# Two gate projections of a mixer: their high and low weight parts ordered pairwise

## The chip, the cores and the metric

The kernel runs on one core of one Trainium2 chip. The metric is the time of one execution on the device in microseconds. Three runs of the kernel before gave 1438.70, 1439.01 and 1439.03, a median of 1439.01.

## The reference

The input x has 256 tokens of 1024 features, all in float32. Two layers of a first kind and one of a second kind follow each other. A layer of the first kind is: a feed-forward block (SwiGLU, inner width 2816), a mixer, and a second feed-forward block. The mixer is what the change touches:

```
h = rms_norm(x, mix_norm)
z = h @ w_in                      # u, q, k, v of 512 columns each, and gl of 2 x 1024
y_pool = multiscale_pool(u, pool_w, pool_scale)
q, k = rope(rms_norm(q)), rope(rms_norm(k))
y_attn = moba_attention(q, k, v)  # 8 heads of 64, causal
gates = sigmoid(gl + b_gate).reshape(B, S, 2, D)
merged = gates[:, :, 0] * (y_pool @ w_branch_pool) + gates[:, :, 1] * (y_attn @ w_branch_attn)
x = x + merged @ w_out
```

With 256 tokens and attention blocks of 256, the attention is plain causal attention over the 256 tokens.

## The kernel before

**Precision.** Every weight tile (128 x 1024 elements) and every activation is split in a high part (float32r) and a low part (what the high part leaves). A product is high x high + high x low + low x high. ScalarE makes the high part of a tile (`whi`, line 1092), VectorE the low one (`wlo`, line 1625). There are 8 raw buffers and 6 of each part. The order of the tiles is a list, and all engines follow it. A semaphore `tile` counts the tiles that TensorE has done with. ScalarE waits for it before it overwrites a buffer, and tables (`HI_LEAD`, `LO_LEAD`) say how many tiles ahead the splits run: for the gate tiles four (ScalarE) and three (VectorE).

**Stages.** Eight stages: `L0f1`, `L0`, `L0f2`, `L1f1`, `L1`, `L1f2`, `M`, `Mf`. `L0` and `L1` are mixers one and two, `M` is a mixer of the second kind, the others are feed-forward blocks.

**A gate.** The gate projections give 2 x 1024 features, for 256 tokens. They are computed by eight feature blocks of 128 (f), each with two gates (j = 0 and 1; called A and B here). `wide_block` of one gate is `high_part` and then `low_part` (lines 556 to 574):

- `high_part` waits for the tile's high weights and issues eight matmuls of 128 x 512 (line 559): the moving operand holds the high and the low activations side by side, so columns 0 to 255 of the bank get high x high and columns 256 to 511 high weights x low activations.
- `low_part` waits for the low weights and issues eight matmuls of 128 x 256 (line 566) into columns 0 to 255, and the last one raises `tile`.

Each gate has a PSUM bank of its own, taken in turn from four (`claim`, banks 0 to 3). A claim waits until VectorE has added up the gate that had the bank before. When a gate is done, ScalarE copies its columns 256 to 511 to `gates` (line 1282, `gate_low`), VectorE adds columns 0 to 255 (line 1921), and ScalarE applies a tanh (line 1288).

**Attention beside it.** The attention of the mixer is spread over the gate blocks by `tick()`. TensorE's `high_part` calls it after its sixth matmul and `low_part` after its last, so a feature block has four ticks. At each call `attention` looks up what falls due (`attention_beat`): the heads come as four pairs. For a pair whose scores are at tick n:

- n: `scores` on TensorE (line 743); VectorE's maxima (lines 1772, 1773); ScalarE's four exponentials (lines 1241, 1242)
- n+2, n+3: `sums` of the first and the second head on VectorE (reciprocal, line 1785; scaling, lines 1791 and 1792)
- n+4, n+5: `turn_p` on TensorE, three transposes of the first and of the second head (line 754). They wait for the scaling of their head, and those of the second head also for ScalarE's eviction of the first (line 1249)
- the product with v (line 769) for two pairs at once, 12 ticks after the scores of the first of them

Counted from the first tick of the first feature block, the scores of the four pairs are at ticks 0, 6, 12 and 18.

ScalarE and VectorE have a fixed program of their own in the same beats. For each gate in turn VectorE does: split of the weight tile three ahead, two ticks, wait for ScalarE's copy, add. ScalarE does: split of the tile four ahead, two ticks, copy of the gate, tanh of the gate before. These two programs are written gate by gate:

```
for f in range(KD):
    for j in range(2):
        ahead(T[f"{tag}g{j}{f}"])
        tick()
        tick()
        g = gates[:, (2 * f + j) * S:(2 * f + j + 1) * S]
        E.wait_ge("g_low", 16 * l + 2 * f + j + 1)
        e.tensor_tensor(g, g, bank[...][:, 0:S], ALU.add).then_inc(sem["g_sum"], 1)
```

The feed-forward stages use the same two functions for their blocks. There most blocks have the parts in the order high, high, low, low (line 711), and the last block of a stage has two `wide_block`s (lines 717, 726).

Of the kernel before, what the change touches and what calls it, by code (L numbers as in the profile page):

```python
# [302 lines left out]
def build_program(nc, x_in, wstream, gains, const_in, par_in, out, cat, pat, plan):  # L303
    K = Counts(plan)
    T, DONE, SI = K.T, K.DONE, K.SI

    with ExitStack() as ctx:
# [98 lines left out]
        def jobs1(l):  # L406

            out_ = []
            for h in range(8):
                c = h // 2  # L410
                out_.append(dict(
                    q=lambda a, b_, c=c, r=64 * (h % 2): qT1[r:r + 64, c * S + a:c * S + b_],
                    k=lambda a, b_, c=c, r=64 * (h % 2): kT1[r:r + 64, c * S + a:c * S + b_],
                    sc=scq.rearrange("p (a h) -> p h a", a=2)[:, h, :], nsc=nscq.rearrange("p (a h) -> p h a", a=2)[:, h, :],
                    v=lambda s, h=h: v1[:, s * 512 + h * 64:s * 512 + h * 64 + 64],
                    gate=None, pair=c, first=True, last=True))
            return out_
# [91 lines left out]
        def pe_program(E):  # L509
# [11 lines left out]
            def claim(name):  # L521
                b, s, v = K.BANK[name]
                E.wait_ge(s, v)
                return bank[b]
# [31 lines left out]
            def high_part(j, b, tick=None):  # L556
                E.wait_ge("w_hi", SI[j] + 1)
                for k in range(KD):
                    e.matmul(b[:, :], hi_of(j)[:, k * P:k * P + P], hx[:, k * 2 * S:k * 2 * S + 2 * S], start=k == 0, stop=False, skip_group_check=True)  # L559
                    if tick and k == 5:  # L560
                        tick()

            def low_part(j, b, tick=None):
                E.wait_ge("w_lo", SI[j] + 1)
                for k in range(KD):
                    ins = e.matmul(b[:, 0:S], lo_of(j)[:, k * P:k * P + P], hiT(k), start=False, stop=k == KD - 1, skip_group_check=True)  # L566
                ins.then_inc(sem["tile"], 1)
                if tick:
                    tick()

            def wide_block(j, b, tick=None):

                high_part(j, b, tick)
                low_part(j, b, tick)
# [31 lines left out]
            def first_group(n, g):  # L606

                groups = a_group(512)
                for i, (k0, m) in enumerate(groups):
                    E.wait_ge("xlo", 4 * n + (1 if k0 < 4 else 2))  # L610
                    last = i == len(groups) - 1
                    group_part(g, 512, T[f"{g}{k0}"], k0, m, 0, claim((g, 0)), (lambda: norm_transposes(n, 1, (0,))) if last else None)
                norm_transposes(n, 1, (1,))
                for i, (k0, m) in enumerate(groups):
                    done = 4 * n + (3 if k0 < 4 else 4)
                    if i:
                        E.wait_ge("xlo", done)
                        group_part(g, 512, T[f"{g}{k0}"], k0, m, 1, claim((g, 1)))
                    else:
                        E.wait_ge("xhi", 4 * n + 3)  # L620
                        group_part_low_last(g, 512, T[f"{g}{k0}"], k0, m, 1, claim((g, 1)), done)

            def group(g, n, tick):
                for k0, m in a_group(n):
                    for a in range(2):
                        group_part(g, n, T[f"{g}{k0}"], k0, m, a, claim((g, a)))
                        tick()
# [155 lines left out]
            def attention(m, b, first, js, before):  # L783
                for what, i in attention_beat(m, b, first, len(js)):
                    if what == "scores":
                        if i == 0:
                            before(0)
                            before(1)
                        scores(m, i, js)
                    elif what == "turn":  # L790
                        turn_p(m, i)
                    elif what == "out":
                        if i == 0:
                            before(2)
                        attend(m, i, js)
                    elif what == "post":
                        attend_compressed(i)

            def turn4(srcs, b):
                for k, s in enumerate(srcs):  # L800
                    ins = e.transpose(b[:, k * P:k * P + P], s, ident)  # L801
                return ins
# [19 lines left out]
            def mixer1(s, l):  # L822
                tag = STAGES[s]
                js = jobs1(l)
                beat = 0

                def turn_qk(a, isq):
                    if isq:
                        E.wait_ge("rp_add", 4 * l + 2 + a + 1)
                        E.wait_ge("kt_ev", 2 * l + a + 1)  # L830
                    else:
                        E.wait_ge("x", 4 * (s - 1) + a + 1)
                        E.wait_ge("rp_add", 4 * l + a + 1)
                        E.wait_ge("ld_c", 16)
                    turn4([ro[:, a * 512 + c * P:a * 512 + c * P + P] for c in range(4)], side[a]).then_inc(sem["qkt_t"], 1)

                def pool_diff(g):
                    E.wait_ge("u_ev", 2 * l + 2)
                    E.wait_ge("ld_pm", 16 * l + 16)
                    E.wait_ge("ld_pw", 16 * l + 16)  # L840
                    if g < 2:
                        E.wait_ge("kt_ev", 2 * l + g + 1)
                    else:
                        E.wait_ge("qt_ev", 2 * l + g - 1)
                        E.wait_ge("dT", 4 * l + g - 1)
                    b, pm = side[g % 2], poolm[:, g * 384:g * 384 + 384]
                    reach = P + 2 ** (g + 1)
                    e.matmul(b[:, 0:reach], us[:, g * P:g * P + P], pm[:, 0:reach], start=True, stop=False, skip_group_check=True)
                    e.matmul(b[:, P:S], us[:, 512 + g * P:512 + g * P + P], pm[:, S:S + P], start=False, stop=True,
                             skip_group_check=True).then_inc(sem["pl_d"], 1)  # L850

                def pool_mix(g):
                    E.wait_ge("dT", 4 * l + g + 1)
                    if g >= 2:
                        E.wait_ge("yplo", 4 * l + g - 1)
                    else:
                        E.wait_ge("x", 4 * (s - 1) + 3 + g)
                    e.matmul(side[2 + g % 2][:, 0:S], pw[:, g * P:g * P + P], dT, start=True, stop=True).then_inc(sem["pl_w"], 1)

                def before(i):  # L860
                    if i < 2:
                        E.wait_ge("dT", 4 * l + 3 + i)
                        E.wait_ge("kt_ev", 2 * l + 2)
                        E.wait_ge("qt_ev", 2 * l + 2)
                        E.wait_ge("yplo", 4 * l + 3)
                    else:
                        E.wait_ge("v_ev", 2 * l + 2)
                        E.wait_ge("yplo", 4 * l + 4)

                def tick():  # L870
                    nonlocal beat
                    beat += 1
                    if beat in (10, 12):
                        turn_qk((beat - 10) // 2, False)
                    if beat in (20, 22):
                        turn_qk((beat - 20) // 2, True)
                    if beat in (17, 19, 21, 23):
                        pool_diff((beat - 17) // 2)
                    if beat in (18, 20, 22, 24):
                        pool_mix((beat - 18) // 2)  # L880
                    attention(l, beat, 25, js, before)

                first_group(s, f"{tag}k")
                for g in ("q", "u", "v"):
                    group(f"{tag}{g}", 512, tick)
                for f in range(KD):
                    for j in range(2):
                        wide_block(T[f"{tag}g{j}{f}"], claim((f"{tag}g", f, j)), tick)
                merge_tail(s, l)

            def mixer2(s):
# [181 lines left out]
            for s, tag in enumerate(STAGES):  # L1073
                if tag in FFNS:
                    ffn(s)
                elif tag == "M":
                    mixer2(s)
                else:
                    mixer1(s, int(tag[1]))
# [1428 lines left out]
```

## Time and profile before

| | |
|---|---|
| median of three runs | 1439.01 us |
| the profiled execution, its own time | 1438.99 us |
| its span, first to last instruction | 1437.1 us |
| TensorE matmuls busy | 1431.4 us (x8064) |
| TensorE weight loads busy | 1232.0 us |
| VectorE busy | 984.7 us |
| ScalarE busy | 802.0 us |
| GpSimd busy | 144.6 us |
| gate blocks of mixer one | 244.98 us to 292 us and on, in the span |

Times are counted from the first instruction of the span. Matmuls overlap, so the start of one to the start of the next is what it takes of TensorE; the duration that a row gives is longer. In the timeline a row merges instructions of one line that follow each other: its start, its length, the engine, the line, the operation, what it writes and reads, and how many there are. In brackets stands how long the engine had been idle before it, and what it waited for.

### The profile page before, as it was taken

Reading aid. Unit: us, or ns where it says so; the run is one execution under the profiler, and the core shown is the slowest. Engines: PE = TensorE matmul, PEld = TensorE weight load, DVE = VectorE, ACT = ScalarE, POOL = GpSimd, SP = SyncE. Lnnn points to the kernel's source line nnn. Section 1 sums busy time; section 2 is a strip of 40 time slices with the busy share of each in tenths; the row PEclk is TensorE's granted clock in tenths of the full one; section 3 lists DMA queues with packets and bytes.
Section 4 is the critical chain, followed back from the end, with each engine's and each line's share of the span. In section 5 each row is a group of like instructions: output and inputs, shape, how many; then the busy total and the mean of one; then the engine's idle time right before and its main releaser. Section 6 shows DMA issues by size and latency. Waiting matters only on the chain.

```text
span 1437.1 us, 20811 instructions
## 1 busy us (share of the span) xinstructions
PE 1431.4 (100%) x8064; PEld 1232.0 (86%) x8064; DVE 984.7 (69%) x1601; ACT 802.0 (56%) x1409; POOL 144.6 (10%) x212
## 2 busy tenths in 40 slices
PE   9999999999999999999999999999999999999999
PEld 7888888898888888888888898888888899888887
DVE  6656676777666566666676677665676977678776
ACT  6545556754555555455566746554557765465553
POOL 0100024000000001000050004000038300100000
PEclk9999999999999999999999999999999999999999
DMA  8655555354655537555564455555546335456551
GB/s 337 246 194 187 191 206 189 133 187 152 233 185 189 196 129 254 188 193 190 176 234 138 159 188 202 181 189 197 195 157 233 132 118 188 164 166 216 192 189 59
DMA packets 73681, 267.76 MB, mean 186 GB/s; under 512 B 8176, under 2 KB 8304, under 8 KB 73456
## 3 DMA queue, kind: packets, MB, share of 16 engines
q1 hardware_dynamic: 73296, 265.65, 54.1%
q8 instruction: 64, 1.05, 0.3%
q10 hardware_dynamic: 288, 0.79, 0.1%
q14 instruction: 33, 0.27, 0.1%
HBM read 265.36 MB, written 1.05 MB: 185 GB/s over the span
## 4 chain that ended last, share of the span: by engine, by line
PE 99%; DMA 0%; DVE 0%; POOL 0%; issue 0%; POOLq 0%
PE bank L559 30%; PE bank L566 15%; PE bank L513 9%; PE bank L514 9%; PE bank L515 8%; PE bank L580 4%; PE bank L587 4%; PE bank L581 4%; PE bank L543 3%; PE bank L550 3%; PE bank L544 3%; PE bank L533 1%; PE bank L743 1%; PE bank L754 1%; PE bank L769 1%; PE bank L801 1%
## 5 line engine op out<-in xcount | busy, mean ns | idle before, releaser
L1625 DVE TENSOR_TENSOR wlo<-raw,whi 128x1024 fp32r<-128x1024 f32 (+1 forms) x481 | 579.6, 1228 | 14.2 <-ACT whi L1092 14.2
L1092 ACT ACTIVATE whi<-raw 128x1024 fp32r<-128x1024 f32 (+1 forms) x481 | 490.0, 1048 | 5.5 <-DMA raw<-w_dram 2.8
L559 PE MATMUL bank<-hx,whi 128*128 128x512 f32 x1856 | 452.4, 392 | 0.0
L559 PEld LDWEIGHTS bank<-hx,whi 128*128 128x128 f32 x1856 | 343.7, 188 | 71.1 <-issue 3.0
L566 PEld LDWEIGHTS bank<-hx,wlo 128*128 128x128 f32 x1856 | 242.0, 191 | 11.6
L566 PE MATMUL bank<-hx,wlo 128*128 128x256 f32 x1856 | 245.5, 282 | 0.0
L513 PE MATMUL bank<-whi,hid 128*128 128x512 f32 x536 | 211.2, 394 | 0.2 <-issue 0.2
L514 PE MATMUL bank<-wlo,hid 128*128 128x512 f32 x536 | 209.9, 392 | 0.0
L515 PE MATMUL bank<-whi,hid 128*128 128x512 f32 x536 | 208.6, 389 | 0.0
L1722 DVE TENSOR_TENSOR sil<-sil,bank 128x256 f32<-128x256 f32 x80 | 33.6, 420 | 182.1 <-ACT sil L1181 182.1
L1181 ACT ACTIVATE sil<-bank 128x256 f32<-128x256 f32 x80 | 30.6, 383 | 211.5 <-PE bank L566 211.5
L1121 ACT ACTIVATE hid<-prod 128x256 fp32r<-128x256 f32 x126 | 52.7, 418 | 169.0 <-DVE prod L1733 110.4
L515 PEld LDWEIGHTS bank<-whi,hid 128*128 128x128 f32 x536 | 100.7, 188 | 21.8
L513 PEld LDWEIGHTS bank<-whi,hid 128*128 128x128 f32 x536 | 101.1, 189 | 17.9 <-issue 0.4
L514 PEld LDWEIGHTS bank<-wlo,hid 128*128 128x128 f32 x536 | 101.1, 189 | 16.3
L580 PE MATMUL bank<-whi,hx 128*128 128x512 f32 (+1 forms) x272 | 108.9, 402 | 0.9 <-DVE hx L1653 0.9
L581 PE MATMUL bank<-whi,hx 128*128 128x512 f32 (+1 forms) x272 | 104.5, 385 | 0.0
L2190 POOL TENSOR_SCALAR small<-small 128x1 f32<-128x1 f32 x16 | 11.0, 688 | 886.5 <-ACT arena L1107 882.0
L1658 DVE TENSOR_TENSOR hid<-prod,hid 128x256 fp32r<-128x256 f32 x126 | 53.6, 425 | 61.0 <-ACT hid L1121 61.0
L587 PE MATMUL bank<-wlo,hx 128*128 128x512 f32 (+1 forms) x272 | 82.8, 387 | 0.0
L580 PEld LDWEIGHTS bank<-whi,hx 128*128 128x128 f32 x272 | 51.1, 188 | 11.3 <-DVE hx L1653 1.6
L587 PEld LDWEIGHTS bank<-wlo,hx 128*128 128x128 f32 x272 | 49.8, 188 | 12.2 <-DVE wlo L1625 2.3
(250 smaller groups left out, 1512.7 us busy)
## 6 DMA issues: line engine op xcount, KB each, us to landing
raw<-w_dram SPq DMA_DIRECT2D x486, 512.0 KB, 3.5
gain<-g_dram SPq DMA_DIRECT2D x7, 512.0 KB, 3.9
arena<-c_dram SPq DMA_DIRECT2D x2, 768.0 KB, 6.3
cst<-c_dram SPq DMA_DIRECT2D x1, 1056.0 KB, 5.9
out_dram<-x SPq DMA_DIRECT2D x4, 256.0 KB, 2.0
par<-p_dram SPq DMA_DIRECT2D x1, 867.0 KB, 7.5
raw<-w_dram SPq DMA_DIRECT2D x2, 432.0 KB, 3.1
gain<-g_dram ACTq DMA_DIRECT2D x1, 512.0 KB, 4.9
```

The costliest lines, as they stand in the source:

```text
L513: e.matmul(psum, shi, mhi, start=first, stop=False, skip_group_check=True)
L514: e.matmul(psum, shi, mlo, start=False, stop=False, skip_group_check=True)
L515: return e.matmul(psum, slo, mhi, start=False, stop=last, skip_group_check=True)
L559: e.matmul(b[:, :], hi_of(j)[:, k * P:k * P + P], hx[:, k * 2 * S:k * 2 * S + 2 * S], start=k == 0, stop=False, skip_group_check=True)
L566: ins = e.matmul(b[:, 0:S], lo_of(j)[:, k * P:k * P + P], hiT(k), start=False, stop=k == KD - 1, skip_group_check=True)
L580: e.matmul(b[:, 0:n], hiT(k, a * P, a * P + P), w, start=k == 0, stop=False, skip_group_check=True)
L581: e.matmul(b[:, 0:n], loT(k, a * P, a * P + P), w, start=False, stop=False, skip_group_check=True)
L587: ins = e.matmul(b[:, 0:n], hiT(k, a * P, a * P + P), w, start=False, stop=k == KD - 1, skip_group_check=True)
L1092: e.activation(hi_of(t), raw_of(t), ACT.Copy).then_inc(sem["w_hi"], 1)
L1121: e.activation(hid[h_ % 4][:, 0:S], src, ACT.Copy).then_inc(sem["hidhi"], 1)
L1625: e.tensor_tensor(lo_of(t), raw_of(t), hi_of(t).bitcast(F32), ALU.subtract).then_inc(sem["w_lo"], 1)
L1658: e.tensor_tensor(hb[:, S:2 * S], src, hb[:, 0:S].bitcast(F32), ALU.subtract).then_inc(sem["hidlo"], 1)
```

## The change

In the gate loop of `mixer1` both banks of a feature block are claimed at its start. Then come the high part of A, the high part of B, the low part of A and the low part of B. Every matmul stays what it was, and so do the number of ticks and the programs of ScalarE, VectorE, GpSimd and SyncE. Mixer three (`mixer2`) is not touched.

```diff
                 for f in range(KD):
+                    tiles, held = [T[f"{tag}g{j}{f}"] for j in range(2)], [claim((f"{tag}g", f, j)) for j in range(2)]
                     for j in range(2):
-                        wide_block(T[f"{tag}g{j}{f}"], claim((f"{tag}g", f, j)), tick)
+                        high_part(tiles[j], held[j], tick)
+                    for j in range(2):
+                        low_part(tiles[j], held[j], tick)
```

TensorE's instructions in the second feature block of mixer one and the start of the third, before. A's bank is 1 and B's is 2; line 559 is the high part, 566 the low part, 754 the transposes, 743 the scores:

```order
L559 MATMUL bank1<-hx,whi 128x512 x6
L754 MATMUL bank6<-cst,arena 128x128 x3
L559 MATMUL bank1<-hx,whi 128x512 x2
L566 MATMUL bank1<-hx,wlo 128x256 x8
L754 MATMUL bank6<-cst,arena 128x128 x3
L559 MATMUL bank2<-hx,whi 128x512 x6
L743 MATMUL bank4<-arena 128x128
L743 MATMUL bank5<-arena 128x128
L743 MATMUL bank4<-arena 128x256
L743 MATMUL bank5<-arena 128x256
L559 MATMUL bank2<-hx,whi 128x512 x2
L566 MATMUL bank2<-hx,wlo 128x256 x8
```

And with the change:

```order
L559 MATMUL bank1<-hx,whi 128x512 x6
L754 MATMUL bank6<-cst,arena 128x128 x3
L559 MATMUL bank1<-hx,whi 128x512 x2
L559 MATMUL bank2<-hx,whi 128x512 x6
L754 MATMUL bank6<-cst,arena 128x128 x3
L559 MATMUL bank2<-hx,whi 128x512 x2
L566 MATMUL bank1<-hx,wlo 128x256 x8
L743 MATMUL bank4<-arena 128x128
L743 MATMUL bank5<-arena 128x128
L743 MATMUL bank4<-arena 128x256
L743 MATMUL bank5<-arena 128x256
L566 MATMUL bank2<-hx,wlo 128x256 x8
```

The second transposes came behind A's low part, and now stand among B's high matmuls. The scores came among B's high matmuls, and now stand between the two low parts. A's last matmul is now behind sixteen high ones.

The third feature block goes on so before (A's bank is 3, B's is 0):

```order
L559 MATMUL bank3<-hx,whi 128x512 x8
L566 MATMUL bank3<-hx,wlo 128x256 x8
L559 MATMUL bank0<-hx,whi 128x512 x6
L754 MATMUL bank6<-cst,arena 128x128 x3
L559 MATMUL bank0<-hx,whi 128x512 x2
L566 MATMUL bank0<-hx,wlo 128x256 x8
L754 MATMUL bank6<-cst,arena 128x128 x3
```

And with the change:

```order
L559 MATMUL bank3<-hx,whi 128x512 x8
L559 MATMUL bank0<-hx,whi 128x512 x8
L566 MATMUL bank3<-hx,wlo 128x256 x8
L754 MATMUL bank6<-cst,arena 128x128 x3
L566 MATMUL bank0<-hx,wlo 128x256 x8
L754 MATMUL bank6<-cst,arena 128x128 x3
```

The first transposes of the pair came among B's high matmuls, and now stand behind A's low part; the second ones still end the block.

VectorE's instructions in the second feature block, the same before and after: the add of gate A (bank 1), a split, and then the maxima of the scores, of which the first three instructions are shown:

```order
L1921 TENSOR_TENSOR gates<-gates,bank1 128x256
L1625 TENSOR_TENSOR wlo<-raw,whi 128x1024
L1772 ISA arena,small<-bank4,cst 128x128
L1772 ISA small 128x1
L1773 ISA arena,small<-bank4,cst 128x256
```

Nothing moved here: the maxima stand behind the add of gate A in both kernels.

## Rows read from the trace of the kernel before

**Rows 1.** The page's chain that ended last, shares by engine.

```profile
PE 99%; DMA 0%; DVE 0%; POOL 0%; issue 0%; POOLq 0%
```

**Rows 2.** Span and mean granted clock of the core.

```profile
core 0: 1437.1 us, clock 1.000
```

**Rows 3.** What TensorE's transposes (line 754) waited for: us in total, times.

```profile
  DVE arena L1792: 2.2, 6
```

**Rows 4.** Timeline of TensorE in stage L0f1: blocks in both orders.

```profile
127.82 3.79 PE L559 MATMUL bank<-hx,whi 128*128 128x512 f32 x16
131.44 2.08 PE L566 MATMUL bank<-hx,wlo 128*128 128x256 f32 x16
133.36 0.40 PE L513 MATMUL bank<-whi,hid 128*128 128x512 f32 x1
...
177.54 1.98 PE L559 MATMUL bank<-hx,whi 128*128 128x512 f32 x8
...
183.10 0.40 PE L513 MATMUL bank<-whi,hid 128*128 128x512 f32 x1
```

**Rows 5.** Timeline of TensorE in mixer one, feature blocks one to four.

```profile
246.65 0.93 PE L743 MATMUL bank<-arena 64*128 64x128 f32 x8
...
251.80 1.55 PE L559 MATMUL bank<-hx,whi 128*128 128x512 f32 x6
253.20 0.49 PE L754 MATMUL bank<-cst,arena 128*128 128x128 f32 x3
...
253.99 1.12 PE L566 MATMUL bank<-hx,wlo 128*128 128x256 f32 x8
254.95 0.49 PE L754 MATMUL bank<-cst,arena 128*128 128x128 f32 x3
...
256.76 0.93 PE L743 MATMUL bank<-arena 64*128 64x128 f32 x8
257.61 0.72 PE L559 MATMUL bank<-hx,whi 128*128 128x512 f32 x2
...
263.42 0.55 PE L754 MATMUL bank<-cst,arena 128*128 128x128 f32 x3
...
265.46 1.64 PE L559 MATMUL bank<-hx,whi 128*128 128x512 f32 x6
```

**Rows 6.** Timeline of ScalarE, same stretch: gate copies and first exponential.

```profile
251.22 0.36 ACT L1282 ACTIVATE gates<-bank 128x256 f32<-128x256 f32 x1
252.00 0.38 ACT L1282 ACTIVATE gates<-bank 128x256 f32<-128x256 f32 x1 [0.42 <-PE bank L566]
...
255.86 0.38 ACT L1282 ACTIVATE gates<-bank 128x256 f32<-128x256 f32 x1
...
258.62 0.49 ACT L1241 ACTIVATE arena<-arena,small 128x128 f32<-128x128 f32 x1 [1.03 <-DVE small L1779]
...
260.75 0.36 ACT L1282 ACTIVATE gates<-bank 128x256 f32<-128x256 f32 x1
```

**Rows 7.** Timeline of VectorE, same stretch: split, maxima, first sum.

```profile
256.61 1.22 DVE L1625 TENSOR_TENSOR wlo<-raw,whi 128x1024 fp32r<-128x1024 f32 x1
257.75 0.28 DVE L1772 CUSTOM_DVE_ANT_0 arena<-bank,cst 128x128 f32<-128x128 f32 x1
...
262.62 0.16 DVE L1785 RECIPROCAL small<-small 128x2 f32<-128x2 f32 x1
```

**Rows 8.** Timeline of all engines, third pair: scores, copy of gate A, transposes.

```profile
268.48 0.93 PE L743 MATMUL bank<-arena 64*128 64x128 f32 x8
...
272.46 0.36 ACT L1282 ACTIVATE gates<-bank 128x256 f32<-128x256 f32 x1
...
275.12 0.55 PE L754 MATMUL bank<-cst,arena 128*128 128x128 f32 x3
```

**Rows 9.** Timeline of TensorE in mixer two: scores and transposes of the second pair.

```profile
777.32 0.93 PE L743 MATMUL bank<-arena 64*128 64x128 f32 x8
...
783.99 0.55 PE L754 MATMUL bank<-cst,arena 128*128 128x128 f32 x3
```

## The prediction

> **What bounds the kernel now.** I read the page first. The chain of work that ended last runs over TensorE for 99% of the span [rows 1]. So only two things can move the time: what TensorE's own instructions take in another order, and the idle time it gets because somebody else is late. The granted clock is 1.000 over the whole span of 1437.1 us [rows 2], its upper level of 2.4 GHz. Next I read who waited for whom. The rows that matter are small: the transposes of the attention weights (line 754) found TensorE six times waiting for VectorE's line 1792, 2.2 us in all [rows 3]. That is the scaling that ends the softmax of a head. It means that this side chain already has no slack at some of its meetings with TensorE. The rest of the working is on the timelines of the three engines through the gate blocks of mixer one.
>
> I call the eight blocks F0 to F7, their two gates A and B, and the four pairs of heads P0 to P3. A block offers four places (ticks) for attention work, and the pairs meet them thus: scores of P0 at F0's first tick and of P1 at F1's third, P2 at F3's first, P3 at F4's third. The transposes of a pair's two heads come four and five ticks after the scores: P0 at F1's first and second tick, P1 at F2's third and fourth, P2 at F4's first and second, P3 at F5's third and fourth. The change keeps the count of ticks and moves them against the matmuls.
>
> **The change, part by part.** *TensorE's own work.* The same 16 high and 16 low matmuls per block are issued, and nothing is added. What goes is one switch from low to high and one back. Stage one of the same kernel has both forms side by side: high A, high B, low A, low B took 127.82 to 133.36, 5.54 us; the form by turns took 177.54 to 183.10, 5.56 us [rows 4]. So a block gains 0.02 us and 16 blocks 0.3 us. Bounds: nothing, and 0.1 us a block where a tick adds a switch. [...] The rows say 0.02 us a block, which I take.
>
> *Late end of gate A.* This is the part that costs. The last low matmul of A comes after B's high ones, so A's result is complete up to 2.2 us later, while B's is complete when it was. ScalarE copies A's bank (line 1282), VectorE adds the other half (line 1921), and both do so in a fixed order which the change doesn't touch. On VectorE the order is: add A, one split of a weight tile (line 1625), the maxima of the scores (line 1772). The maxima of P1 and P3 therefore stand behind gate A of the same block. In F1, from the rows of before:
> - F1 starts at 251.80. The transposes come at 253.20 as before, and these with two high matmuls take 0.79 (to 253.99) [rows 5]. Then six high matmuls of B: 6 x 3.62/16 = 1.36 [rows 4], to 255.35; second transposes and two matmuls 0.79, to 256.14; A's low part 0.96 [rows 5], to 257.10. It was 254.95.
> - ScalarE starts a copy 0.20 after a gate's end when it is free (252.00 against 251.80) [rows 5, 6], so at 257.30 in place of 255.86: 1.44 later.
> - From that copy to the maxima is 257.75 - 255.86 = 1.89 [rows 6, 7]: 259.19. From maxima to the first exponential 0.87, to the copy behind the four exponentials 2.13 more [rows 6, 7]: 262.19. From this copy over the add and a split to the sums (line 1785) 1.87: 264.06 [rows 6, 7]. From the sums to TensorE's transposes 263.42 - 262.62 = 0.80 [rows 5, 7]: 264.86. They were at 263.42.
> - TensorE, unhindered, would come there earlier: scores at 257.10, +0.85 (256.76 to 257.61) [rows 5], B's low part 0.96, which ends F1 at 258.9; F2's 16 high ones 3.62 and a low part 0.96: 263.5. It **waits 1.3 to 1.4 us**.
> - From the transposes to F3's start was 265.46 - 263.42 = 2.04, with two high matmuls (0.45) in it that now lie ahead: 1.59. F3 starts at 266.45, not 265.46. So F1 and F2 together cost **+1.0 us**, the switches saved already in it.
>
> P3 in F4 and F5 has the same ticks and the same queue: +1.0 us. Bounds of each: +0.5, if one step of the chain (the split, 1.14 from start to start [rows 7]) falls into a pause that I haven't seen; +1.5, if TensorE also has to wait at the second transposes, behind ScalarE's eviction of the first.
>
> *P2.* Its scores are at F3's first tick. Before, ScalarE copied F3's gate A straight behind the exponentials, 272.46 - 268.48 = 3.98 after the scores, and the transposes began 6.64 after them [rows 8]. Now A ends scores 0.85 + ten high matmuls 2.26 + low 0.96 = 4.07 after the scores, some 0.1 more for the switches, and its copy can start at +4.3. So VectorE's sums behind A are 0.3 to 0.4 later, TensorE was already waiting there, and this is path: **+0.35 us**, bounds 0 and 0.6.
>
> *P0.* The same place in F0, but the exponentials there start late (a table load stands ahead), so ScalarE reaches gate A at 251.22 in any case [rows 6]. A now ends 4.17 after the scores at 246.65 [rows 5], at 250.8, and its copy could start at 251.0. Nothing, with 0.2 us to spare.
>
> *Weights and banks.* B's high tile is wanted 0.96 us earlier than before, and A's buffers are given back up to 2.2 us later. ScalarE splits four tiles ahead and waits for the release of the tile two before the one it is at, which lies behind a copy it has already made; so no new wait. VectorE's splits, and with them the DMA issues on SyncE's queue that wait for them, move with VectorE by at most 1.5 us, against a lead of at least three tiles of 2.8 us each. Both banks are now claimed at a block's start; they were freed by the sums two blocks before, which even late are done some 3 us ahead (F1's B is added at 262.6, F3 starts at 266.4). I cost all this at nothing; if the cover were gone it would be a wait on the weight splits ahead of a block.
>
> **Sum.** Per mixer 1.0 + 0.35 + 1.0 = 2.35, less 0.02 for each of the other four blocks: 2.3. Mixer two runs the same code, and its P1 took 777.32 to 783.99, 6.67 us, against 256.76 to 263.42, 6.66 us [rows 5, 9]. Two mixers: +4.6 us. The profiled execution took 1438.99 us, which is the median 1439.01 for this purpose: **1443.6 us**, 0.3% slower. The bounds of the terms give per mixer 2 x 0.5 + 0 - 0.1 = 0.9 to 2 x 1.5 + 0.6 = 3.6, in all 1440.8 to 1446.2; I don't expect all ends at once.
>
> **Rivals.**
> - *No wait arises (not slower).* Place: P1's transposes in F2 and P3's in F5. If the chain from copy A to the sums were 1.4 us shorter than I add up, TensorE would arrive last, and the small waits of [rows 3] would go too: 1439.0 - 0.3 - up to 0.5, about 1438.3 us. It decides at the point where VectorE's scaling ends before 263.5 (F1 counted as above). For it: the new order moves the transposes a little later. Against: by 0.1 us only, while the maxima move by 1.4, and [rows 3] show that there was no slack. 0.11.
> - *Half of it.* Only P1 and P3 count and by half each, 1440.7 us. 0.09.
> - *The clock gives way.* So far the granted clock is 1.000 [rows 2]. If it fell to its lower level (1.2 GHz) for a block after each of the four waits, each would cost another 5.5 us, since a block's matmuls would take twice 5.5: up to 1465 us. Against it: 6 small waits left the clock alone, and the gap of 1.3 us is short beside a block. The Trainium skill ("TensorE: Matmul & The Clock Gate", section "A second HAM failure mode: psum-queue depth-cycling") reports a kernel in which small idle times between groups of matmuls brought the clock down again and again. By that rule this rival would hold; the trace here, with its six waits at clock 1.000, does not show it. 0.03.
>
> **How the numbers follow.** My forecast has 0.77. A measurement of this kernel can tell about 0.2% from no change, 2.9 us, so the border is at 1441.9 and 1436.1. Faster has only the first rival's far end: 0.02. Within: the rest of the first rival, most of the second, and a little of the forecast's low end: 0.16. Slower: 0.82. The range takes the forecast's likely part and reaches down to the half case: 1440.5 to 1445.6.
>
> **What would show it.** TensorE's weight loads of line 754 should wait for VectorE's line 1792 four times for over 1 us (P1 and P3, both mixers) and twice for about 0.5 us (P2). P1's transposes should start some 13.0 us after F1's start, not 11.6. VectorE's maxima of P1 should follow gate A's add and one split. Matmul counts and durations stay. The prediction is wrong if the transposes find their input ready, if the waits come at the weight splits (lines 1092, 1625) instead, or if the granted clock is below 1.000 in the gate blocks.

## The result, and the profile after

The changed kernel takes 1444.11 us (median of 6 runs, 1443.80 to 1444.34), the kernel before 1439.01. The ratio is 1.0036 with a 95% interval of 1.0026 to 1.0046: slower by 5.1 us. The forecast was 1443.6 us in a range of 1440.5 to 1445.6.

The profiled execution took 1444.15 us. Its span and clock answer to [rows 2], the shares of the chain that ended last to [rows 1]:

```profile
core 0: 1442.3 us, clock 1.000
```

```profile
PE 96%; DVE 2%; ACT 1%; DMA 1%; SPq 0%; issue 0%
```

The clock is unchanged. The span is 5.2 us longer, and TensorE's part of the chain has gone from 99% to 96%, with VectorE and ScalarE taking 3% together. The lines of ScalarE and VectorE stand 3 higher here than before (1249 is 1252, 1282 is 1285, 1625 is 1628, 1792 is 1795, 1921 is 1924), since the change adds three lines above them. The lines of TensorE named here stay the same.

Who TensorE's matmuls waited for (total us, times, longest):

```profile
PE bank L754 <- DVE arena L1795: 4.7, 6, 1.0
```

Six waits: four of 0.99 us and two of 0.38; the next fence shows the three of mixer one. [rows 3] gave 2.2 us for six in a view that counts weight loads and matmuls; the same view now says 11.1 us for twelve, six of each.

The timeline of TensorE through the first seven feature blocks of mixer one, which answers to [rows 5, 8]. The starts of F0, F1, F2, F3, F4 and F6 are 245.08, 251.93, 259.26, 266.60, 274.79 and 290.06:

```profile
245.08 1.74 PE L559 MATMUL bank<-hx,whi 128*128 128x512 f32 x6
...
251.93 1.55 PE L559 MATMUL bank<-hx,whi 128*128 128x512 f32 x6
253.32 0.49 PE L754 MATMUL bank<-cst,arena 128*128 128x128 f32 x3
...
255.50 0.49 PE L754 MATMUL bank<-cst,arena 128*128 128x128 f32 x3
...
257.35 0.93 PE L743 MATMUL bank<-arena 64*128 64x128 f32 x8
...
259.26 3.82 PE L559 MATMUL bank<-hx,whi 128*128 128x512 f32 x16
...
265.02 0.55 PE L754 MATMUL bank<-cst,arena 128*128 128x128 f32 x3 [0.99 <-DVE arena L1795]
...
266.60 1.64 PE L559 MATMUL bank<-hx,whi 128*128 128x512 f32 x6
...
269.62 0.93 PE L743 MATMUL bank<-arena 64*128 64x128 f32 x8
...
274.79 1.55 PE L559 MATMUL bank<-hx,whi 128*128 128x512 f32 x6
276.72 0.55 PE L754 MATMUL bank<-cst,arena 128*128 128x128 f32 x3 [0.38 <-DVE arena L1795]
...
290.06 1.63 PE L559 MATMUL bank<-hx,whi 128*128 128x512 f32 x6
```

From F1 to F3 it is now 14.67 us (266.60 - 251.93), where 13.66 stood: +1.01. From F3 to F6 it is 23.46, where it was 287.44 - 265.46 = 21.98: +1.48. F0 takes 6.85, before 6.82. The whole stretch of six blocks, as the view of busy time by window gives it, after and before (columns: window, length, and for TensorE's matmuls, its weight loads, VectorE, ScalarE and GpSimd the busy us and the count, then clock, DMA share, GB/s):

```profile
245.08:290.06 44.98, 42.61 (x266) 35.01 (x265) 28.41 (x88) 33.30 (x76) 0.00 (x0) 1.00 0.37 126
```

```profile
244.98:287.44 42.46, 42.46 (x267) 34.56 (x265) 28.84 (x88) 32.80 (x76) 0.00 (x0) 1.00 0.39 136
```

44.98 less 42.46 is 2.52 us. Mixer two has the same waits at the same places, so two mixers give 5.04 of the 5.1 us. TensorE's busy time differs by 0.15 us (42.61 against 42.46); the rest is idle time at three transposes.

Which chain it is, the chain that ended last says itself for the first of them. Its pieces between gate A's end in F1 and the first transposes of P1, start and length:

```profile
257.45 0.39 ACT gates L1285
...
257.87 0.42 DVE gates L1924
258.29 1.14 DVE wlo L1628
259.43 0.20 DVE arena L1775
...
260.21 0.59 ACT arena L1244 x2
...
262.45 0.28 ACT gates L1285
...
263.17 1.13 DVE wlo L1628
...
264.70 0.27 DVE arena L1795
...
265.02 0.55 PE bank L754 x3
```

To be read: ScalarE copies gate A (1285), VectorE adds it (1924) and splits a weight tile (1628), and only then come the maxima (1775, 1776), the four exponentials (1244, 1245), the copy of gate B (1285), its add, another split (1628), the scaling of the first head (1795) and the transposes at 265.02.

### The profile page after: what moved, and what is told of

Same layout as the page of the kernel before. It is cut to its first block, busy times and chain, and to the rows that moved or that the text cites. A ratio compares the mean times of both kernels' runs of the same rounds, so it can differ in the third digit from the quotient of the medians.

```text
span 1442.3 us, 20797 instructions
## 1 busy us (share of the span) xinstructions
PE 1431.8 (99%) x8064; PEld 1233.0 (85%) x8064; DVE 984.8 (68%) x1601; ACT 802.3 (56%) x1409; POOL 144.5 (10%) x212
## 3 DMA queue, kind: packets, MB, share of 16 engines
q8 instruction: 64, 1.05, 0.3%
HBM read 265.36 MB, written 1.05 MB: 185 GB/s over the span
## 4 chain that ended last, share of the span: by engine, by line
PE 96%; DVE 2%; ACT 1%; DMA 1%; SPq 0%; issue 0%
PE bank L559 28%; PE bank L566 15%; PE bank L513 9%; PE bank L514 9%; PE bank L515 8%; PE bank L580 4%; PE bank L587 4%; PE bank L581 4%; PE bank L543 3%; PE bank L550 3%; PE bank L544 3%; PE bank L533 1%; PE bank L754 1%; PE bank L769 1%; DVE wlo L1628 1%; PE bank L743 1%
```

## The experiments

The theory: the end of gate A, which the new order puts up to 2.2 us later, holds VectorE and ScalarE, whose programs are fixed, and through them the attention's transposes. The rival: the new matmul order has a price of its own, per block. Each kernel below was timed beside the kernel before, whose median was 1439.0 in each set (1438.71 to 1439.42 over all of its runs).

| kernel | median us | range | against before |
|---|---|---|---|
| the change | 1444.11 | 1443.80 to 1444.34 | +5.1 |
| new order in F0, F2, F5, F6, F7 | 1442.92 | 1442.79 to 1443.01 | +3.9 |
| new order in F1, F4 | 1445.08 | 1444.79 to 1445.13 | +6.1 |
| new order in F3 | 1439.98 | 1439.70 to 1440.23 | +1.0 |
| new order in F0, F6, F7 | 1438.93 | 1438.70 to 1439.35 | 0.0 |
| change, VectorE's splits behind the ticks | 1442.93 | 1442.61 to 1443.09 | +3.9 |
| change, ScalarE's splits behind the ticks | 1450.58 | 1448.44 to 1453.82 | +11.6 |
| change, both | 1438.78 | 1438.55 to 1439.20 | -0.2 |
| change, third tick ahead of gate A's copy and add | 1441.38 | 1441.22 to 1441.90 | +2.4 |
| the same, and VectorE's splits behind the ticks | 1438.13 | 1437.84 to 1438.48 | -0.9 |
| before, VectorE's splits behind the ticks | 1438.07 | 1437.86 to 1438.47 | -0.9 |
| before, both | 1438.16 | 1437.86 to 1438.31 | -0.8 |

### In which blocks the cost lies

Four kernels choose the blocks that get the new order; the others keep `wide_block`:

```diff
                 for f in range(KD):
+                    if f not in (0, 2, 5, 6, 7):
+                        for j in range(2):
+                            wide_block(T[f"{tag}g{j}{f}"], claim((f"{tag}g", f, j)), tick)
+                        continue
...
```

The other three have (1, 4), (3,) and (0, 6, 7) in that place.

New order in F0, F2, F5, F6 and F7. Expected: 

> High, high, low, low only in feature blocks F0, F2, F5, F6 and F7 of both mixers; F1, F3 and F4 by turns as before. My theory (a late end of gate A holds VectorE's maxima and sums, only in F1, F3 and F4): none of the long waits, 1438.4 us; the transposes of P1 and P3 find their input ready or almost. Rival (the new matmul order itself is slow, or both banks claimed early make TensorE wait): 10 of 16 blocks changed, so about 10/16 of the 5.1 us, 1442.2 us.

Measured 1442.92. The theory as it stood falls here: it allowed 1438.4. By count of blocks 1442.2 was expected, so this run alone speaks for the rival. The waits of TensorE say what happened:

```profile
PE bank L754 <- ACT arena L1256: 4.0, 4, 1.0
```

Four waits of 1.0 us again, but for ScalarE's line 1256, which is the eviction of the first transposes (1249 in the kernel before). The second transposes wait for it, since they overwrite what it reads. ScalarE in F2:

```profile
263.99 0.38 ACT L1289 ACTIVATE gates<-bank 128x256 f32<-128x256 f32 x1 [1.47 <-PE bank L566]
264.27 0.50 ACT L1295 ACTIVATE gates<-gates,small 128x256 f32<-128x256 f32 x1
264.67 1.05 ACT L1099 ACTIVATE whi<-raw 128x1024 fp32r<-128x1024 f32 x1
265.62 0.48 ACT L1256 ACTIVATE arena<-bank 128x384 f32<-128x384 f32 x1
```

ScalarE copies gate A of F2 first (263.99), then does a tanh and a split, and the eviction comes at 265.62, although the transposes that it evicts began at 263.79. So there is a second chain, in F2 and F5: gate A's late end, copy, tanh, split, eviction, second transposes.

New order in F1 and F4. Expected: 

> The new order only in F1 and F4 (4 of 16 blocks). My theory: the chain from gate A's end fixes the time of P1's and P3's transposes, wherever they stand in F2 and F5. These blocks are by turns again, so two high matmuls and a switch lie behind the transposes that lay ahead of them: F1 to F3 costs 14.65 + 0.45, which is 1.4 us over before, four times: 1444.8 us, more than the whole change. Rival (cost by count of changed blocks): 4/16 of 5.1 us, 1440.3 us.

Measured 1445.08: a quarter of the blocks costs more than all of them, as the theory said and the rival can't. The scores of P1 and the first transposes in this kernel:

```profile
257.35 0.93 PE L743 MATMUL bank<-arena 64*128 64x128 f32 x8
...
265.03 0.55 PE L754 MATMUL bank<-cst,arena 128*128 128x128 f32 x3 [1.42 <-DVE arena L1799]
```

The transposes are at 265.03, against 265.02 with the whole change: their time is set by the chain from F1, not by the order in F2. They wait 1.42 us in place of 0.99, and in F2 two high matmuls are still to come behind them.

New order in F3 alone. Expected: 

> The new order only in F3. My theory: gate A's copy comes 0.35 to 0.45 us later behind the exponentials of P2, so its transposes wait about 0.8 us instead of 0.3: 1439.8 us. Rival (P2's wait grew for another reason, such as the delay handed on from F2): 1439.0 us.

Measured 1439.98, +1.0 in two mixers, 0.5 for each P2. The ratio's interval, 0.9997 to 1.0015, just takes in no change, but the runs (1439.70 to 1440.23) lie above all of before's.

New order in F0, F6 and F7. Expected: 

> The new order only in F0, F6 and F7, where no transposes wait behind gate A. The matmul order itself costs nothing: 1438.9 us, within 0.3 us of before. Rival (the order has a price of its own, 6 of 16 blocks): 1440.5 us or more.

Measured 1438.93. Six of sixteen blocks, no transposes behind their gate A, no cost and no gain; the six small waits of [rows 3] are there as before (2.2 us). The rival is out.

### Taking links out of the chains

The next kernels leave TensorE's order as the change has it and move other work. VectorE's splits behind the two ticks of their gate:

```diff
                     for j in range(2):
-                        ahead(T[f"{tag}g{j}{f}"])
                         tick()
                         tick()
+                        ahead(T[f"{tag}g{j}{f}"])
```

Expected: 

> The changed kernel, with VectorE's split of a weight tile moved behind the two ticks of each gate (in both mixers). My theory: the split, 1.14 us, stands in the chain from gate A's add to the maxima and once more ahead of the sums; without it the six waits of the transposes vanish, the transposes stand 0.2 us later in the block with two high matmuls less behind them: 1438.0 us, at or under the kernel before. Rival (the wait comes from ScalarE's side or from the matmul order): nothing or 1.2 us less, 1443 to 1444 us. A third: the splits come late and TensorE waits for low weights, over 1444 us.

Measured 1442.93, not 1438.0. The waits for VectorE are gone, and the second chain holds alone:

```profile
PE bank L754 <- ACT arena L1252: 4.1, 4, 1.0
```

Line 1252 is ScalarE's eviction in this kernel. Four waits of 1.0 us again, in place of four of 0.99 and two of 0.38. The kernel with the new order in F0, F2, F5, F6 and F7 had cut the first chain by leaving F1 and F4 alone, this one cuts it by its split, and both end at 1442.9: there are two chains of almost one length, and without the first the second still costs 3.9 of the 5.1 us.

Both engines' splits behind the ticks (the same edit in ScalarE's program too). Expected: 

> The changed kernel with both engines' weight splits moved behind the two ticks of each gate. Theory, mended: two chains of nearly one length hold TensorE at P1's and P3's transposes; VectorE's (gate A's add, split, maxima) holds the first ones, ScalarE's (gate A's copy in F2 and F5, a split, then the eviction of the first transposes) holds the second. With both shortened no wait over 0.2 us is left: 1437.8 us, under the kernel before. Rival (another thing holds TensorE, such as the late release of A's buffers): over 1441 us.

Measured 1438.78, which is 0.2 under before and 1.0 over the number forecast. Against the kernel before with both splits moved in the same way (1438.16, further down) 0.6 us of the 5.1 is left. ScalarE's eviction in F2 now comes straight behind the tanh:

```profile
263.63 0.39 ACT L1285 ACTIVATE gates<-bank 128x256 f32<-128x256 f32 x1
263.92 0.50 ACT L1291 ACTIVATE gates<-gates,small 128x256 f32<-128x256 f32 x1
264.31 0.48 ACT L1252 ACTIVATE arena<-bank 128x384 f32<-128x384 f32 x1
```

The splits as the middle link of both chains are thus shown: 5.3 us hang on where they stand, of which 0.8 us is gained in the kernel before too. What is left over 1438.1 I take to be the rest of the eviction chain, since A's low part between the transposes takes 1.26 us here in F2 (263.68 to 264.94) and 1.18 in F5 (285.65 to 286.83), and 1.05 in the last of the changed kernels, in which no transposes wait (263.76 to 264.81). In two mixers that makes 0.7 us. It wasn't tried further.

ScalarE's splits alone. Expected: 

> The changed kernel with ScalarE's split alone moved. Theory of two chains: VectorE's still holds the first transposes; ScalarE's split now stands between the exponentials and the copy of gate B, ahead of the sums, so this chain gets up to 0.95 us longer: 1444 to 1448 us. Rival (ScalarE's chain is the only one that counts): 1440 us or less.

Measured 1450.58, more than 2 us above the end of what was expected, and with the widest range of all (1448.44 to 1453.82). The direction is the theory's: the split now stands between the exponentials and the copy of gate B, on VectorE's chain, and the first transposes of P1 and P3 wait 1.95 us, 0.96 longer than with the change. P2's wait grew too, from 0.38 to 0.87, which the expectation left out. Four times 0.96 and twice 0.49 are 4.8 us. The one run whose mean granted clock was 1.000 took 1448.44, 4.3 over the change; the others had a lower clock, as the section on the hardware below shows.

The third tick of a block ahead of gate A's copy and add, on both engines, as TensorE itself now has it:

```diff
                 for f in range(KD):
+                    ahead(T[f"{tag}g0{f}"])
+                    tick()
+                    tick()
+                    ahead(T[f"{tag}g1{f}"])
                     for j in range(2):
-                        ahead(T[f"{tag}g{j}{f}"])
-                        tick()
                         tick()
```

Expected: 

> The changed kernel with ScalarE and VectorE following TensorE's new order: the block's third tick stands ahead of gate A's copy and add, the splits stay ahead of the ticks. Theory: the maxima start 1 us after the scores as before, and P2's sums no longer stand behind gate A, so P2's wait goes. P1 and P3: behind the exponentials now come both copies and both adds and a split before the sums, so the first transposes come at about 264.7 in place of 265.0, a wait of 0.8 us in place of 1.2; ScalarE evicts ahead of gate A's copy, so no second wait. 1444.1 less 4 x 0.3 less 2 x 0.45: 1442.0 us. Rival (the add of gate A ahead of the maxima is the whole cost): 1438.5 us.

Measured 1441.38. VectorE's timeline in F1 and F2:

```profile
257.93 0.29 DVE L1777 CUSTOM_DVE_ANT_0 arena<-bank,cst 128x128 f32<-128x128 f32 x1 [2.91 <-PE bank L743]
...
261.35 0.42 DVE L1928 TENSOR_TENSOR gates<-gates,bank 128x256 f32<-128x256 f32 x1 [1.77 <-ACT gates L1285]
262.01 0.42 DVE L1928 TENSOR_TENSOR gates<-gates,bank 128x256 f32<-128x256 f32 x1 [0.25 <-ACT gates L1285]
262.35 1.22 DVE L1630 TENSOR_TENSOR wlo<-raw,whi 128x1024 fp32r<-128x1024 f32 x1
263.49 0.16 DVE L1790 RECIPROCAL small<-small 128x2 f32<-128x2 f32 x1
```

The maxima start at 257.93, 0.95 behind the scores, and no longer behind gate A. Both adds and a split (1630) now stand behind the exponentials. F1 starts at 251.56 in this profile and at 251.93 in that of the change, so the sums come 11.93 us after it in place of 12.29 (264.22 - 251.93). That is the small gain at P1 and P3 which was expected: their waits are 0.63 and 0.72 us. P2's wait is gone. The rival is out: gate A's add is behind the maxima, and the four waits still make 2.6 us.

The same, with VectorE's splits behind the ticks. In a block VectorE then does: two ticks, split, third tick, split, add of A, fourth tick, add of B; ScalarE's program is that of the last kernel. Expected: 

> As the last one, with VectorE's splits behind the ticks: the split leaves the way to P1's and P3's sums, 1.14 us, which is more than the 0.8 us wait left there. No wait over 0.2 us: 1438.3 us. If the splits were not in the chain: 1442 us like the last one.

Measured 1438.13, and no transposes wait. The new matmul order with no wait left costs what the old one costs without waits, as the last two show.

### The kernel before without its small waits

VectorE's splits behind the ticks in the kernel before. Expected: 

> The kernel before with only VectorE's split behind the ticks. By turns, gate A ends early, so ScalarE's eviction chain has slack and needs no shortening; VectorE's does. Theory: as with both splits moved, 1438.1 to 1438.3 us. Rival (ScalarE's part of the gain with both moved is its own): 1438.6 us or more.

Both engines' splits. Expected: 

> The kernel before (gates by turns) with both splits moved behind the ticks. Its six small waits of 0.3 to 0.4 us on the weight-load side go, some 0.15 us of path each: 1438.1 us. Rival (they are hidden): 1439.0 us. With the run of the changed kernel and both splits moved it says what the new matmul order is worth without any wait: 0.0 to 0.4 us.

Measured 1438.07 and 1438.16. With VectorE's splits moved none of the six waits of [rows 3] is left; with both moved eight shorter ones stand there, 1.4 us in all, and the time is the same. So VectorE's part is all of the gain, if it is one: every run of either lies under every run of before, by medians 0.9 and 0.8 us, but the ratio of each is 0.9994, with intervals of 0.9985 to 1.0003 and 0.9985 to 1.0002, and by the interval the gain isn't established. These two and the last of the changed kernels are the fastest of the study, at 1438.1 us each.

## Why the prediction was right

- *TensorE's own work.* Forecast -0.3 us in all. The order without waits is worth nothing that these runs can tell: 1438.93 against 1438.96 in F0, F6 and F7, and 1438.13 against 1438.07 with all blocks. In the profiles of the latter two F1 to F5 take 35.21 us (251.57 to 286.78) and 35.23 (251.66 to 286.89). So the 0.02 us a block that I read from stage one doesn't show here; F0, with a tick in it, even took 0.03 more. The Trainium skill ("TensorE: Matmul & The Clock Gate", section "Back-to-back issue gap") gives an isolated matmul of N columns N/2.4 + 2.5 ns at the full clock, about 216 ns for 512, and about 131 ns in a stream with weight loads. The rows are near the first and far from the second: sixteen matmuls of 512 columns with their weight loads take 3.62 us, 226 ns each [rows 4].
- *P1 and P3.* Forecast +1.0 each, measured +1.01 (F1 to F3) and +1.02 (from P2's first transposes to F6, 13.34 against 12.32). The steps of the chain hold one by one. Forecast were gate A's copy at 257.30, the maxima at 259.19, the copy of B at 262.19 and the sums at 264.06; measured are 257.45, 259.34, 262.35 and 264.22, in a profile that runs 0.13 later at F1's start. The transposes were forecast 13.06 after F1's start (264.86 - 251.80), measured 265.02 - 251.93 = 13.09. What was off is TensorE's own way to them. Two low parts take 1.05 and 1.06 us (256.30 to 257.35, 258.20 to 259.26) where the prediction has 0.96, and the view counts a wait from the end of the last matmul's row. So the matmuls waited 0.99 us, not 1.3 to 1.4. That leaves the sum alone, since the chain and not TensorE sets the time of the transposes.
- *P2.* Forecast +0.35, measured 1.93 - 1.46 = 0.47 from F4's start to the transposes, and 0.5 in the kernel with F3 alone. This is the mis-sized term: 0.12 in each mixer, about half of the 0.5 us by which the sum fell short of 1444.1. The other half is in small parts: no gain in the four other blocks (F0 took 0.03 more, F3 8.19 against 8.20), and 0.01 and 0.02 at P1 and P3.
- *The sign to look for.* The weight loads of line 754 were to wait four times for over 1 us and twice for about 0.5. They waited 1.20 and 0.81, as the rows of F2 and F4 in the changed kernel show (PEld is TensorE's weight load):

```profile
265.02 0.31 PEld L754 LDWEIGHTS bank<-cst,arena 128*128 128x128 f32 x3 [1.20 <-DVE arena L1795]
...
276.71 0.31 PEld L754 LDWEIGHTS bank<-cst,arena 128*128 128x128 f32 x3 [0.81 <-DVE arena L1795]
```

- *P0, weights and banks.* Costed at nothing. F0 and the kernel with F0, F6 and F7 show nothing, nor does the last of the changed kernels, which claims both banks early in all blocks.
- *The rivals.* Waits arose at full size, so "no wait" (1438.3) and "half" (1440.7) are out. The clock stayed at 1.000 in all six runs.
- *What it missed.* The second chain, ScalarE's eviction. The prediction had it as the upper bound of P1's term. It is in fact a hair shorter than the first: in the changed kernel the eviction starts at 265.69, takes 0.48, and is done 0.2 us before TensorE comes to the second transposes at 266.36. It is hidden while the first holds, and it doesn't change the sum. It does change what one gains by mending only one: my expectations for two runs were 4.5 and 4.9 us too low because of it.

## What to carry to other kernels

When TensorE's work is reordered, the count of its instructions says little; ask when each result is complete, and which engine has the reading of that result in its fixed queue ahead of something that TensorE waits for later. Look for the second chain of nearly the same length before expecting the gain of cutting the first. A side job with a lead of several tiles, as these splits have, belongs behind the work with a deadline: in the changed kernel that gave 5.3 us, with no instruction added or removed, when it was done on both engines at once. On VectorE alone it gave 1.2, and on ScalarE alone it cost 4.3 at an unchanged clock and 6.5 in the median.

## What the runs showed of the hardware

With ScalarE's splits moved alone, TensorE's matmuls waited 1.95 us in F2 of mixer one, and the granted clock fell. Busy time by window of that kernel (the columns as above; the clock is the number before the DMA share):

```profile
262.00:265.50 3.50, 1.55 (x12) 1.27 (x10) 2.24 (x6) 3.21 (x6) 0.00 (x0) 1.00 0.00 0
265.50:267.70 2.20, 2.20 (x15) 2.20 (x15) 2.03 (x5) 0.49 (x1) 0.00 (x0) 0.69 0.71 238
267.70:270.30 2.60, 2.60 (x10) 1.84 (x10) 0.48 (x2) 2.11 (x4) 0.00 (x0) 0.60 0.59 202
270.30:275.00 4.70, 4.70 (x35) 3.50 (x36) 2.65 (x11) 1.50 (x6) 0.00 (x0) 1.00 0.34 112
```

The clock is 1.00 through the wait, 0.69 and 0.60 in the 4.8 us behind it, and 1.00 again. These are means over stretches with both levels, 1.2 and 2.4 GHz: from 266.5 to 269.5 alone the same view gives 0.50, the lower one. Six high matmuls took 2.5 us there, from 267.69 to 270.21. In mixer two a wait of the same 1.95 us left the clock alone, and six took 1.57 (794.04 to 795.61). The transposes, A's low part behind them and the six matmuls, in mixer one and in mixer two:

```profile
265.50 0.55 PE L754 MATMUL bank<-cst,arena 128*128 128x128 f32 x3 [1.95 <-DVE arena L1795]
265.80 1.60 PE L566 MATMUL bank<-hx,wlo 128*128 128x256 f32 x8
...
267.69 2.59 PE L559 MATMUL bank<-hx,whi 128*128 128x512 f32 x6
```

```profile
792.46 0.55 PE L754 MATMUL bank<-cst,arena 128*128 128x128 f32 x3 [1.95 <-DVE arena L1795]
792.76 1.19 PE L566 MATMUL bank<-hx,wlo 128*128 128x256 f32 x8
...
794.04 1.64 PE L559 MATMUL bank<-hx,whi 128*128 128x512 f32 x6
```

From the transposes to the start of F3 it is 2.19 us with the lower clock (267.69 - 265.50) and 1.58 without, and the six matmuls of F3 take 0.95 more: 1.6 us for this one fall.

The other runs bear this out. Time and mean granted clock of the five runs of this kernel:

| us | clock |
|---|---|
| 1448.44 | 1.000 |
| 1449.92 (the profiled one) | 0.999 |
| 1450.58 | 0.999 |
| 1452.15 | 0.997 |
| 1453.82 | 0.996 |

Every run of every other kernel has 1.000. So the clock fell in four of the five runs, more in some than in others, and the time follows it: this is the scatter of 5.4 us, where the other kernels scatter over 0.7 at most. Which waits the falls stand behind is seen in the profiled run alone.

The changed kernel's waits of 0.99 us brought the clock down in none of its six runs, whose means are 1.000, nor did the six waits of before, in which only the weight loads were idle. The Trainium skill ("TensorE: Matmul & The Clock Gate", section "A second HAM failure mode: psum-queue depth-cycling") says that idle time between groups of matmuls can do this; in the profile here it did so behind one wait of 1.95 us out of four. So the rival that the prediction gave 3% is a thing that happens in a near relative of the changed kernel, but not in the changed kernel.
